# mLSTM gate rows: running maxima by two scans on VectorE in place of 16 score matrices and their row maxima

## What is computed

```python
b = jnp.cumsum(lf.reshape(B, H, nc, CHUNK), axis=-1)
tri = jnp.tril(jnp.ones((CHUNK, CHUNK), dtype=bool))
logd = jnp.where(tri, b[..., :, None] - b[..., None, :] + igc[..., None, :], -jnp.inf)
m_inter = b + m0[..., None]
m_t = jnp.maximum(m_inter, jnp.max(logd, axis=-1))
w_inter = jnp.exp(m_inter - m_t)
s = jnp.einsum('bhctd,bhcsd->bhcts', qc, kc) * jnp.exp(logd - m_t[..., None])
```

## Time and profile before

| | us |
|---|---|
| median of 3 runs | 2563.54 |
| lowest, highest | 2562.18, 2578.25 |
| the profiled execution's own time | 2562.28 |
| its span, first to last instruction | 2560.5 |
| PE busy in the span | 2333.3 |
| DVE busy | 739.4 |
| ACT busy | 418.9 |

### The profile page before, as it was taken

One profiled execution on the slowest core, in us unless ns is written; L12 is line 12 of the kernel. 1 busy time (PEld: TensorE's weight loads), 2 busy tenths in 40 slices (PEclk: granted clock), 3 DMA queues, 4 the chain that ended last, 5 costly groups with the idle time before them and its releaser, 6 DMA issues.

```text
span 2560.5 us, 75374 instructions
## 1 busy us (share of the span) xinstructions
PE 2333.3 (91%) x33826; PEld 2005.0 (78%) x33826; DVE 739.4 (29%) x2049; ACT 418.9 (16%) x883; POOL 0.2 (0%) x4
## 2 busy tenths in 40 slices
PE   4979899987999989999999999999979796699996
PEld 3746788876744679999999999999968465577775
DVE  5566644323277320001000000100041244422223
ACT  1022100010144221111011111111121311211111
POOL 0000000000000000000000000000000000000000
PEclk7956999967899989999999999999999978699999
DMA  9330888632334359999999999999951000099994
GB/s 340 129 134 28 315 298 315 248 115 80 132 132 151 146 181 394 352 394 345 394 347 394 345 361 380 345 394 347 394 222 66 1 1 0 7 381 407 407 407 176
DMA packets 253002, 640.76 MB, mean 250 GB/s; under 512 B 15104, under 2 KB 21376, under 8 KB 247680
## 3 DMA queue, kind: packets, MB, share of 16 engines
q1 hardware_dynamic: 252080, 634.93, 66.3%
q10 hardware_dynamic: 848, 4.84, 0.5%
HBM read 638.68 MB, written 1.05 MB: 250 GB/s over the span
## 4 chain that ended last, share of the span: by engine, by line
PE 83%; DVE 7%; DMA 7%; ACT 2%; issue 1%; DVEq 0%; ACTq 0%
PE psum L668 35%; PE psum L464 8%; DMA ring<-in_w_up 6%; PE psum L578 3%; PE psum L565 3%; PE psum L587 3%; PE psum L765 3%; PE psum L521 3%; PE psum L547 3%; PE psum L455 2%; PE psum L436 2%; PE psum L531 2%; PE psum L648 1%; PE psum L421 1%; PE psum L966 1%; PE psum L1116 1%
## 5 line engine op out<-in xcount | busy, mean ns | idle before, releaser
L668 PE MATMUL psum<-uT,ring 128*64 128x96 f32 x14336 | 601.3, 246 | 0.0
L668 PEld LDWEIGHTS psum<-uT,ring 128*64 128x64 f32 x14336 | 594.6, 137 | 0.1
L668 PE MATMUL psum<-arena,ring 128*64 128x96 f32 x7168 | 305.2, 246 | 0.0
L668 PEld LDWEIGHTS psum<-arena,ring 128*64 128x64 f32 x7168 | 299.1, 137 | 0.0
L1574 DVE TENSOR_TENSOR arena<-arena,psum 128x288 f32<-128x288 f32 x56 | 25.5, 455 | 755.8 <-PE psum L668 755.8
L1447 DVE SCALAR_TENSOR_TENSOR arena<-ring,cact,arena 128x512 f32<-128x512 f32 x196 | 147.4, 752 | 7.0
L1242 ACT ACTIVATE arena<-psum 128x384 f32<-128x384 f32 x56 | 27.5, 491 | 738.1 <-PE psum L668 738.1
L464 PE MATMUL psum<-uT,ring 128*128 128x256 f32 (+1 forms) x496 | 112.5, 388 | 6.3 <-ACT uT L1163 6.3
L464 PEld LDWEIGHTS psum<-uT,ring 128*128 128x128 f32 (+1 forms) x496 | 95.6, 193 | 24.5 <-ACT uT L1163 6.7
L464 PE MATMUL psum<-arena,ring 128*128 128x256 f32 x384 | 89.1, 394 | 9.9 <-ACT uT L1163 9.5
L464 PEld LDWEIGHTS psum<-arena,ring 128*128 128x128 f32 x384 | 75.8, 199 | 21.7 <-ACT uT L1163 9.9
(11 more groups left out here) (346 smaller groups left out, 2516.7 us busy)
## 6 DMA issues: line engine op xcount, KB each, us to landing
ring<-in_moe_w_gate SPq DMA_DIRECT2D x224, 512.0 KB, 7.1
ring<-in_moe_w_up SPq DMA_DIRECT2D x224, 512.0 KB, 5.9
ring<-in_moe_w_down SPq DMA_DIRECT2D x224, 512.0 KB, 7.3
ring<-in_w_ada SPq DMA_DIRECT2D x36, 2048.0 KB, 13.7
ring<-in_w_gate SPq DMA_DIRECT2D x19, 2048.0 KB, 10.9
ring<-in_w_up SPq DMA_DIRECT2D x19, 2048.0 KB, 11.4
ring<-in_w_down SPq DMA_DIRECT2D x19, 2048.0 KB, 10.0
ring<-in_ffn_w_gate SPq DMA_DIRECT2D x5, 2048.0 KB, 8.5
```

Source lines behind the costliest of these rows:

```text
L668: mm = pe.matmul(out(HD * hc), w[:, c0 + HD * hc:c0 + HD * hc + HD], x, skip_group_check=True, **kw)
```

## The change

On DVE, two scans are added behind L1886. They take the running maximum of `rstd`, one forward into `ahead` (over `igr`, which is not needed any more), one over the reversed row into `back` (over `lfr`). A subtraction and a multiply-add with `bwd` (0 for the forward rows, 1 for the backward) select the one that belongs to each row, and `s_lat` is raised only behind these. In gcols PE transposes this row too, two more transposes, and DVE copies 16 more columns to `cols[:, 64:80]`. The 16 jobs r1 go, on PE and on DVE.

```diff
             for t in range(NT):
                 pe.transpose(b[:, 8 * t:8 * t + 8], t1r[0:8, 1, P * t:P * t + P], ident[0:8, 0:8])
                 pe.transpose(b[:, 16 + 8 * t:24 + 8 * t], br_[0:8, 0, P * t:P * t + P], ident[0:8, 0:8])
+                pe.transpose(b[:, 40 + 8 * t:48 + 8 * t], igr[0:8, 0, P * t:P * t + P], ident[0:8, 0:8])
...
-            for j in range(8):
-                for t in range(NT):
-                    b, _ = open_job(pe, "r1", "V")
-                    gate_scores(b, j, t).then_inc(res, 1)
...
-            V(tt(rstd[R, :], igr[R, 0, :], br_[R, 0, :], ALU.subtract), s_lat)
+            V(tt(rstd[R, :], igr[R, 0, :], br_[R, 0, :], ALU.subtract))
+            ahead, back = igr[R, 0, :], lfr[R, 0, :]
+            V(dve.tensor_tensor_scan(ahead, root[R, :], rstd[R, :], TAKEN, ALU.mult, ALU.max))
+            V(dve.tensor_tensor_scan(back[:, ::-1], root[R, :], rstd[R, ::-1], TAKEN, ALU.mult, ALU.max))
+            V(tt(back, back, ahead, ALU.subtract))
+            V(stt(ahead, back, pk("bwd")[R], ahead, ALU.mult, ALU.add), s_lat)
             b = next_job(dve, "gcols", "V")
             gc = small[:, 5:8, 16:32]
             V(dve.tensor_copy(gc[:, 0:2, :], b[:, 0:32].rearrange("p (a n) -> p a n", a=2)))
+            V(dve.tensor_copy(cols[:, 64:80], b[:, 40:56]))
             V(dve.tensor_copy(gc[:, 2, 0:8], b[:, 32:40]), dve_took)
             wk, bcol, m0 = gc[:, 0, :], gc[:, 1, :].rearrange("p (t n) -> p t n", t=2), gc[:, 2, 0:8]
-            for j in range(8):
-                for t in range(NT):
-                    b = next_job(dve, "r1", "V")
-                    s0, s1 = srange(j, t)
-                    ins = dve.tensor_reduce(cols[:, 64 + 8 * t + j:65 + 8 * t + j], b[:, 0:s1 - s0], AX, ALU.max)
-                    N(ins, dve_took)
```

## The result

The changed kernel takes 2534.72 us in the median of 4 runs (2532.81 to 2535.97), the kernel before 2562.86 in the median of the 4 runs beside it (2561.37 to 2578.25). The ratio is 0.9876, interval 0.9838 to 0.9914. Two repetitions with more runs gave 0.9883 (0.9854 to 0.9913) and 0.9876 (0.9852 to 0.9900). So the gain is some 30 us or 1.2%; the forecast was 27.3 us or 1.07%. The total can't settle more than that. The forecast as a ratio, 0.9893, lies inside all three intervals, the first two medians differ by 28.1 us where their ratio says 31.8, and one of the four runs before took 2578.25. The profiled span fell by 29.5 us, from 2560.5 to 2531.0.

A forecast was written before the change was run, and what follows sets the result against it. PE at its low clock was taken to bound the removed stage. 2562.3 - 26.95 + 0.3 = 2535.6 us on the profiled execution's scale, 2536.2 us as median; the forecast's own range was 2532.5 to 2540, for 8 in 10 2532 to 2544.

The forecast's parts named there:

- Removed, added, sum: Score-matrix stage: 29.62 us removed, 2.24, 0.2 and 0.23 added; first keys and c0 26.95 us earlier.
- The clock in c0: PE's clock in the context products c0 climbs 4 to 7 us after their start, within c0's own 8 us.
- the term of 0.3: Cost in us put on a later clock climb in c0, at most 1.3.
- The rule of the page against the row: Removed stage: the skill says activity releases PE's clock, the trace row shows 0.50 to the end; forecast followed the row.
- r1's going takes nothing away: Ahead of c0: the removed matrices did not lift the clock in 30 us, so c0 loses nothing without them.
- Rival 3: Later stages meet the climb differently or an added operation costs its upper bound; 2538 to 2542 us, chance 0.09.
- such shifts go both ways and cancel over runs: Stages behind the loop: clock shifts of 1 to 2 us, argued against the rival of later losses.
- every later stage the same length: Profile after the change: stages behind the output loop keep their length.
- Rival 2: Output loop stays at the low clock, 33 to 41 us longer; 2569 to 2577 us in all, chance 0.03.
- Rival 1: c0 ends before the clock climbs, one to three loop pairs run cold; 2539 to 2548 us, chance 0.08.

The follow-up runs named there:

- e4_full_rows: As e1_r1_back, but the 8-row first matmul of each restored matrix is replaced by one using all 128 rows; median 2550.70 us, ratio 0.9945.
- e1_r1_back: The changed kernel with the 16 score matrices and their row maxima put back ahead of c0, results unread; median 2565.94 us, ratio to before 1.001.
- e2_scans_x3: The changed kernel with each of the two added scans made three times; median 2537.35 us, ratio 0.989.
- e3_pause: The changed kernel with 16 more scans on VectorE between c0 and the output loop, so PE pauses; median 2549.74 us.
- e7_scans_x2: The changed kernel with each of the two added scans made twice; median 2539.94 us, ratio 0.9899.
- e5_split: The changed kernel with gcols no longer waiting for the latent rows, selection behind the second weighted key, new transposes in their own job; median 2536.54 us, ratio 0.9899.

## Why the prediction was right or wrong

**Removed, added, sum: right.** The first keys and c0 came 26.84 us earlier by the forecast's 26.95 (scans 0.68 each; `s_lat` 2.37 later for 2.34; transposes 0.21 for 0.2; copy 0.23). The one row that was off is the selection, 0.47 for 0.41. All three unseen operations lay near the row that was taken, none near its bound.

**The clock in c0: right.** It climbed 4.0 us into c0, as "4 to 7 us" had it, and the term of 0.3 was -0.1.

**The rule of the page against the row: right.** The Trainium skill, "TensorE: Matmul & The Clock Gate", Part 1 ("What's actually happening"), says that activity releases the clock. e4_full_rows agrees (0.50, then 0.99 after 5.3 us) and e1_r1_back doesn't (0.50 through 30.1 us): PE was busy in both, and only the full-row matmuls lifted it. The step "r1's going takes nothing away" holds for c0, which climbed after 4.0 us without r1 ahead of it and after 4.4 with it.

**Rival 3 and the step "such shifts go both ways and cancel over runs": wrong.** This is where the prediction failed. It put what the later stages do at nothing for the forecast and at a loss of some us in the rival, and expected "every later stage the same length". Measured is a gain of 5.1 us behind the loop's start in the mean of three profiles of each kernel (475.2 to 470.1), in two parts. The first, 1.9 us up to the routing table (2.6 between the two first profiles), is PE's clock, and it doesn't cancel over runs: the changed kernel has 53 us at the low clock there in each of three profiles, the kernel before 57 to 60, and e2_scans_x3 with 2.8 us of delay gets the 60 us and the old length back. The second, 3.1 us in the second mixture, is not explained by PE's clock: it has 12, 25 and 18 us at the low clock in the profiles of the kernel before (331.8, 332.0 and 332.3 us long) and 22, 18 and 12 in those of the changed kernel (329.7, 329.7 and 327.3). The sum placed this part rightly, as moving with the table, but gave it no change in length; why it came out shorter stays open, and so does whether that belongs to the change.

26.84 + 0.1 + 5.1 = 32.0 us, and the ratio of 0.9876 is 31.8. That they agree so well is luck, because the intervals reach 6 to 10 us to each side and the gate row's place varies by 16. It is luck too that the first median came within 1.5 us of the forecast's 2536.2, since no term of the sum stood for the later stages.

**Rival 2: the mechanism weaker than priced.** The loop does start cold after a pause and lifts the clock only after 21.6 us. But a cold pair costs 2.65 us more and not 4.1: eight would be 21 us, less than the 27 gained. At this price it would not have ended on the slower side. The price was too high for q times k, 1.28 us for the pair and not 1.87 (taken from the rows of r1, where the matmuls follow each other more slowly), for three transposes, 0.64 and not 1.05 (from the first attention), and for five products, 2.14 and not 2.6 (from c0); the scores cost some 3.5 as against 3.74.

**Rival 1** did not occur in the changed kernel. In e1_r1_back, where the matrices stand ahead of c0, the climb came only at c0's end and cost 1.0 us, within the 1.3 that the prediction allowed.

## What to carry to other kernels

Price a PE stage at the clock that its own window shows, and look at how many rows of the array its matmuls use. A stage of matmuls with a tiny contraction may be twice as dear as its column count suggests (here 29.3 us, with full rows 12.7), and replacing it by a few vector operations on the rows themselves is then worth more. Where several later stages climb from the low clock, a change of a few microseconds ahead of them can move the time of an untouched stage by 2 to 3 us, and repeating the run does not average that away. So compare stage by stage in the trace, beside the granted clock of each, and don't judge an edit of 2 us by the total.

## What the runs showed that was not expected

- A PE that the trace shows as busy can stay at the low clock. Matrices whose first matmul uses 8 rows stayed at 0.50 for 30 us, full-row ones climbed after 5.3 us (e1_r1_back, e4_full_rows), and the output loop, which mixes both with transposes, climbed after 21.6 us (e3_pause) but holds 1.00 once it has it.
- 8-row and full-row fp32 matmuls in turn follow each other after 0.72 us, full-row ones after 0.43, both of 128 columns at the low clock.
- The price of a small edit is not its own time. From the first gate row on, a delay of 2.8 us cost 6.9 us (e2_scans_x3), one of 1.8 cost 6.5 (e7_scans_x2), and bringing the first keys 2.6 us forward cost 3.7 (e5_split), one profile each.
- The time at the low clock tells the length of the stretch up to the routing table in all 14 profiles, but not that of the second mixture, whose chain of waits goes through transfers.
- Single runs scatter by the second attention: how long the clock stays low there goes with a first gate row at 2034 or at up to 2050 us.
- A running maximum by scan costs on 8 rows what a running sum does, 0.68 us for 256 elements, forward or reversed.
